# Rows of 1024 floats instead of 1040 for the activations of the second block

## The chip, the cores and the metric

The kernel runs on one core of a Trainium2 chip, as one program on five engines: TensorE (matmuls), ScalarE, VectorE, GpSimd and the queues that issue transfers (SyncE above all). The metric is the device time of one execution in microseconds; before and after are each the median of several executions.

## What is computed

Two transformer blocks follow each other on a sequence of 1024 tokens of 1024 channels, in float32.

```
x = first_block(x, ...)     # 16 meta tokens in front (1040 rows); 2 layers of:
                            #   rmsnorm, h @ w_in, differential and forgetting attention, @ w_out
x = second_block(x, ...)    # 1024 rows; 1 layer of:
  h_lat = modulate(rms_norm(x, g_mix_pre), sh_a, sc_a)
  proj = h_lat @ w_in       # q, k, v, g: retention over 4 heads;  f: 2-D Fourier mix over 4 groups
  mix = concatenate([ret, fourier_mix(f)]) @ w_out
  x = x + gt_a * rms_norm(mix, g_mix_post)
  u = modulate(rms_norm(x, g_ffn_pre), sh_f, sc_f) @ w_up      # 1024 x 1024 @ 1024 x 5632
  a, b = split(depthwise conv of width 3 over u)
  x = x + gt_f * rms_norm((silu(a) * b) @ w_down, g_ffn_post)  # 1024 x 2816 @ 2816 x 1024
```

## The kernel before

Every large product is made in a split form: each float32 operand is stored as a rounded high part and a remainder, both as float32r, and `mm3` (L960) issues three matmuls for each tile, high x high, high x low and low x high, all through `mm` (L957, the matmul itself is L958). On-chip memory holds the activations in two tiles, AH (high) and AL (low), each of 128 partitions x 8 rows x L floats with L = 1040, since the first block has 16 meta tokens before the 1024 tokens. Row k holds channels 128k to 128k+127 (one a partition) for all tokens. Behind AH and AL lie W32 (two slots of 1024 floats, where weights land), WH and WL (two slots of 1024 floats each, their high and low parts), small tiles of 480 floats in all, and then what each block carves for itself: in the Fourier stage YH begins 11,040 floats into that, and YL 5,120 floats after YH. The second block works on 1024 tokens, and uses columns 0 to 1023 of the same AH and AL.

All engines follow one static order. Weights come in the order of a list (`PLAN`): a DMA into W32, ScalarE makes WH, VectorE makes WL, and TensorE waits for the semaphore `w_lo`. PSUM banks are handed out by `banks`. Every stage of the second block that the change touches:

- **Mixer and Fourier input** (`tensor_chunk`, called by `project` in `tensor_mixer` and in `tensor_fourier`): for 16 + 4 weight slices of 128 columns and two halves of 512 tokens, 8 rows k x 3 matmuls. The weight slice is stationary, 512 tokens of row k of AH or AL move. GpSimd (copy into AH) and VectorE (remainder into AL) write the normalised input before.
- **Output projection** (`tensor_out` with the name "out2"): 128 tokens of row k are stationary, 256 columns of the weight move. ScalarE (`hi`) and VectorE (`lo`) write its input.
- **Up-projection** (`tensor_chunk` and, for part of the first slice, `right`, in pieces of 256 tokens): 44 weight slices x two halves of tokens, 24 matmuls each, weight stationary and activations moving. GpSimd and VectorE write the input (`ffn_fill`).
- **Down-projection** (`product`): the gated values n = 0 to 43 (22 rows, for two halves of the output) pass through the eight rows of AH and AL in turn, row `ai = (FT * half + k) % 8`. 128 tokens of that row are stationary, 512 weight columns move. k is the outer loop and the token tile t the inner one, 24 matmuls for a k, except for the last 4 k of the second half, where t is outside.

Between the mixer's products and the output projection stands a Fourier stage (`rows` in `tensor_fourier`) with other tiles, YH and YL, as the stationary operands and WH and WL moving; for each group six matmuls of 512 columns with two of 2 columns between them. The context's projection uses views CAH and CAL of tiles KH and KL. Neither is touched by the change. The first block goes on using AH and AL as they are.

Of the kernel before, what the change touches and what calls it, by code (L numbers as in the profile page):

```python
# [12 lines left out]
SEQ = 1024  # L13
# [79 lines left out]
def build(nc, A, S, O):  # L93

    ctx = ExitStack()
    with ctx:
# [14 lines left out]
        PSf = PS[:, :, :].rearrange("p a b -> p (a b)")  # L111
        AH = sb("AH", [128, KT, L], F32R)
        AL = sb("AL", [128, KT, L], F32R)
        W32 = sb("W32", [128, 2, 1024])
        WH = sb("WH", [128, 2, 1024], F32R)
        WL = sb("WL", [128, 2, 1024], F32R)
# [888 lines left out]
        def tensor_chunk(e, w, key, c, n, freed_by, among, end):  # L1005
            t = split_slot(w)
            wh = WH[:, t, :].rearrange("p (k m) -> p k m", k=KT)
            wl = WL[:, t, :].rearrange("p (k m) -> p k m", k=KT)
            b, free = banks.take(key, freed_by, among)
            for cc, kk in free or ():  # L1010
                e.wait_ge(*cc.at(kk))
            e.wait_ge(*w_lo.at(w))
            for k in range(KT):
                m = mm3(e, bank(b)[:, 0:n], wh[:, k, :], wl[:, k, :], AH[:, k, c:c + n], AL[:, k, c:c + n], k == 0, k == KT - 1)
            m.then_inc(*gemm_mm.mark(key))
            if end:
                W_OVER[w] = (gemm_mm, key)
# [363 lines left out]
        def tensor_fourier(e):  # L1381

            def take(key, freed, among):
                b, free = banks.take(key, freed, among)
                for c, k in free or ():
                    e.wait_ge(*c.at(k))
                return b

            def columns(g, among=ALL):

                out = []
                for nt in range(0, 4, 2):
                    b = take(("cd", g, nt), [(cd_lo, (g, nt))], [x for x in among if x not in out])
                    out.append(b)
                    if g == 0 and nt == 0:
                        e.wait_ge(*cd_in.at("all"))
                    e.wait_ge(*folded.at(g))
                    for i in range(2):
                        c, o = 128 * (nt + i), bank(b)[:, 256 * i:256 * i + 256]
                        mm(e, o[:, 0:128], FTt[:, g, c:c + 128], CD[:, 0:128], True, True)  # L1400
                        m = mm(e, o[:, 128:256], FO[:, g, c:c + 128], CD[:, 128:256], True, True)
                    m.then_inc(*cd_mm.mark((g, nt)))
                return out

            def start_rows(g, among):

                even[g] = take(("even", g), [(es, g)], among[:1])
                odd[g] = take(("odd", g), [(y_v, g)], among[1:])

            def rows(j, g):  # L1410

                w = WI["dft", j]
                s = split_slot(w)
                oe, oo = bank(even[g]), bank(odd[g])
                if j == 0:
                    e.wait_ge(*cd_lo.at((g, 2)))
                if g == 0:
                    e.wait_ge(*w_lo.at(w))
                ah, al = YH[:, j, g, 0:128], YL[:, j, g, 0:128]
                bh, bl = YH[:, j, g, 128:256], YL[:, j, g, 128:256]  # L1420
                mm3(e, oo, bh, bl, WH[:, s, 512:1024], WL[:, s, 512:1024], j == 0, False)
                mm(e, oo[:, 0:2], ah, ALT, False, False)
                mm(e, oo[:, 0:2], al, ALT, False, j == 3)
                m = mm3(e, oe, ah, al, WH[:, s, 0:512], WL[:, s, 0:512], j == 0, j == 3)
                if j == 3 or g == 3:
                    m.then_inc(*dft_mm.mark((j, g)))
                W_OVER[w] = (dft_mm, (j, 3))

            def middle(g):

                e.wait_ge(*fo_out.at(("mid", g)))
                mm(e, bank(even[g]), CD[:, 0:128], F5[:, g, :], False, False)
                mm(e, bank(odd[g])[:, 0:1], CD[:, 0:128], F5[:, g, 0:1], False, False)

            even, odd = {}, {}
            for g in range(4):
                for ci, (c, n) in enumerate(CH2):
                    tensor_chunk(e, WI["fou", g], ("fou", g, ci), c, n, [(fo_out, (g, ci))], ALL, ci == 1)
                    if g and ci == 0:
                        columns(g - 1)  # L1440
            for g in range(3):
                free = sorted((b for b in ALL if b not in list(even.values()) + list(odd.values())), key=lambda b: banks.taken[b])
                start_rows(g, free[:2])
                rows(0, g)
            last = columns(3, [b for b in ALL if b not in list(even.values()) + list(odd.values())])
            for g in range(3):
                rows(1, g)
            start_rows(3, last)
            rows(0, 3)
            rows(1, 3)  # L1450
            for g in range(4):
                middle(g)
            for j in (2, 3):
                for g in range(4):
                    rows(j, g)

            def first(kt):
                return [(y_lo, kt)]
            tensor_out(e, "out2", [128 * t for t in range(8)], first, lambda q, p: (mix_dve, (q, p)),
                       middle=lambda i: tensor_norm_fill(e, "ffn", i - 2, [b for b in ALL if b != banks.place["out2", 2, i]]) if i >= 2 else None)  # L1460
            tensor_norm_fill(e, "ffn", 2, [b for b in ALL if b not in (banks.place["out2", 2, 3], banks.place["out2", 3, 3])])

        def tensor_ffn(e):
            place = {}

            def right(ab, i):
# [8 lines left out]
                wh, wl = (x(w).rearrange("p (k m) -> p k m", k=KT) for x in (high, low))  # L1475
                c = slice(512 + 256 * i, 768 + 256 * i)
                for k in range(KT):
                    m = mm3(e, bank(place[ab])[:, 256 * i:256 * i + 256], wh[:, k, :], wl[:, k, :], AH[:, k, c], AL[:, k, c],
                            k == 0 and i == 0, k == KT - 1)
                if i == 1:  # L1480
                    m.then_inc(*gemm_mm.mark(key))
# [14 lines left out]
            for half in range(2):  # L1496
                held = [banks.take(("down", half, t), [(down_act if t % 2 else down_dve, t)] if half == 0 else None, ALL) for t in range(8)]

                def product(t, k):
# [12 lines left out]
                    if k == 0:  # L1512
                        for c, x in free or ():
                            e.wait_ge(*c.at(x))
                    m = mm3(e, bank(b), AH[:, ai, 128 * t:128 * t + 128], AL[:, ai, 128 * t:128 * t + 128],
                            WH[:, s, wv], WL[:, s, wv], k == 0, k == FT - 1)
                    if k == FT - 1 or t == 7:
                        m.then_inc(*down_mm.mark((half, k, t)))
# [44 lines left out]
        def scalar(e):  # L1563
# [372 lines left out]
            def fourier():  # L1936
# [24 lines left out]
                e.wait_ge(*mx_in.at("all"))  # L1961

                def hi(g, src):
                    e.activation(AH[:, g, 0:SEQ], src, ACT.Copy).then_inc(*y_hi.mark(g))

                for g in range(4):
                    hi(g, MX[:, g, :])
# [69 lines left out]
            def first_rows(side, a=0, b=4):  # L2037

                e.wait_ge(*g_v.at((3, 1)))
                c = slice(512 * side, 512 * side + 512)  # L2040
                for n in range(a, b):
                    e.activation(AH[:, n, c], G[:, n, c], ACT.Copy).then_inc(*g_hi.mark((side, n)))

            def ffn():
                e.wait_ge(*cw_in.at(0))
# [26 lines left out]
                for half in range(2):  # L2072
                    for k in range(FT):
                        if k % 2 == 0:
                            split_to(WI["down", half, k] + 1)
                        while n <= min(FT * half + k + 3, 2 * FT - 1):
                            kk = n % FT
                            if n >= 8:
                                p = n - 8
                                e.wait_ge(*down_mm.at((p // FT, p % FT, 7)))  # L2080
                            e.activation(AH[:, n % 8, 0:SEQ], G[:, kk, :], ACT.Copy).then_inc(*g_hi.mark(n))
                            n += 1
                        if half and 1 <= k <= 8:
                            t = k - 1
# [50 lines left out]
        def vector(e):  # L2135
# [373 lines left out]
            def lat_fill(p):  # L2509
                c = 256 * p  # L2510
                for k in range(KT):
                    e.wait_ge(*lat_hi.at((p, k)))
                    e.tensor_tensor(AL[:, k, c:c + 256], TBc[:, k % 4, :], f(AH[:, k, c:c + 256]), ALU.subtract).then_inc(*fill_lo.mark(("lat", p, k)))  # L2513

            def between_blocks(add, gain):
                add(0)
# [200 lines left out]
            def fourier():  # L2717
# [10 lines left out]

                def lo(g, src):
                    e.wait_ge(*y_hi.at(g))  # L2730
                    e.tensor_tensor(AL[:, g, 0:SEQ], src, f(AH[:, g, 0:SEQ]), ALU.subtract).then_inc(*y_lo.mark(g))

                for g in range(4):
                    split_to(WI["fou", g] + 1)
# [84 lines left out]
            def ffn_fill(p):  # L2819
                for k in range(KT):  # L2820
                    e.wait_ge(*lat_hi.at(("ffn", p, k)))
                    c = 256 * p
                    e.tensor_tensor(AL[:, k, c:c + 256], TBf[:, (8 * p + k) % 4, :], f(AH[:, k, c:c + 256]), ALU.subtract).then_inc(
                        *fill_lo.mark(("ffn", p, k)))

            def first_rows(side, a=0, b=4):
                c = slice(512 * side, 512 * side + 512)
                for n in range(a, b):
                    e.wait_ge(*g_hi.at((side, n)))
                    e.tensor_tensor(AL[:, n, c], G[:, n, c], f(AH[:, n, c]), ALU.subtract).then_inc(*g_lo.mark((side, n)))  # L2830

            def ffn():
                e.wait_ge(*cw_in.at(0))
# [33 lines left out]
                for half in range(2):  # L2867
                    for k in range(FT):
                        if k % 2 == 0:
                            split_to(WI["down", half, k] + 1)  # L2870
                        while n <= min(FT * half + k + 3, 2 * FT - 1):
                            kk = n % FT
                            e.wait_ge(*g_hi.at(n))
                            e.tensor_tensor(AL[:, n % 8, 0:SEQ], G[:, kk, :], f(AH[:, n % 8, 0:SEQ]), ALU.subtract).then_inc(*g_lo.mark(n))
                            n += 1
                        if half and k == 12:
                            gate_rows(GAf, J2f, 1)
# [35 lines left out]
        def gpsimd(e):  # L2913
# [81 lines left out]
            for p in range(4):  # L2995
                for k in range(KT):
                    e.wait_ge(*fill_tb.at(("lat", p, k)))
                    e.tensor_copy(AH[:, k, 256 * p:256 * p + 256], TBc[:, k % 4, :]).then_inc(*lat_hi.mark((p, k)))
            for t in range(8):
                e.wait_ge(*scaled.at(("lat", t)))  # L3000
                e.tensor_scalar(HT[:, t, :], HT[:, t, :], R12[:, 0, t:t + 1], None, ALU.mult).then_inc(*lat_hi.mark(("x0", t)))
# [25 lines left out]
            def ffn_fill(p):  # L3027
                for k in range(KT):
                    e.wait_ge(*fill_tb.at(("ffn", p, k)))
                    e.tensor_copy(AH[:, k, 256 * p:256 * p + 256], TBf[:, (8 * p + k) % 4, :]).then_inc(*lat_hi.mark(("ffn", p, k)))  # L3030

            residual(0)
            residual(1)
# [187 lines left out]
```

## Time and profile before

| | |
|---|---|
| median of 3 runs | 2876.15 us (2875.58 to 2883.48) |
| the profiled execution, its own time | 2872.7 us |
| its span, first to last instruction | 2870.9 us |
| granted TensorE clock, mean over the span | 0.99 |
| second block, roughly | from 1660 us to the end |
| up-projection | 2142 to 2619 us |
| down-projection | from 2619.5 us to the end |

The profile is of one execution. An engine's busy time is the union of its instructions' durations; for matmuls the durations overlap, because they are pipelined and their ends are modelled, and so the distance from one start to the next is what a matmul occupies. In the rows below `PS<-WH,AH` names the output, the moving operand and the stationary operand, in this order.

### The profile page before, as it was taken

Reading aid. Unit: us, or ns where it says so; the run is one execution under the profiler, and the core shown is the slowest. Engines: PE = TensorE matmul, PEld = TensorE weight load, DVE = VectorE, ACT = ScalarE, POOL = GpSimd, SP = SyncE. Lnnn points to the kernel's source line nnn. Section 1 sums busy time; section 2 is a strip of 40 time slices with the busy share of each in tenths; the row PEclk is TensorE's granted clock in tenths of the full one; section 3 lists DMA queues with packets and bytes.
Section 4 is the critical chain, followed back from the end, with each engine's and each line's share of the span. In section 5 each row is a group of like instructions: output and inputs, shape, how many; then the busy total and the mean of one; then the engine's idle time right before and its main releaser. Section 6 shows DMA issues by size and latency. Waiting matters only on the chain.

```text
span 2870.9 us, 43103 instructions
## 1 busy us (share of the span) xinstructions
PE 2785.9 (97%) x17460; PEld 2402.8 (84%) x17460; DVE 1528.2 (53%) x2774; ACT 1044.9 (36%) x1986; POOL 203.8 (7%) x295
## 2 busy tenths in 40 slices
PE   6999999999999999999999989999999999999999
PEld 5888888888899888888888978888998888888887
DVE  5766555555446666644545475553465444444335
ACT  5434333333334444333334561223352222223232
POOL 1100000000001011000002060000030000000000
PEclk9999999999999999999999999999999999999999
DMA  5221222221322122222214122112231111111113
GB/s 135 48 69 50 69 59 59 61 54 62 120 67 60 53 71 69 63 58 72 65 30 146 58 92 78 52 45 95 97 109 52 52 45 52 45 51 45 52 59 139
DMA packets 205396, 198.10 MB, mean 69 GB/s; under 512 B 7286, under 2 KB 181686, under 8 KB 205198
## 3 DMA queue, kind: packets, MB, share of 16 engines
q1 hardware_dynamic: 187344, 134.27, 17.7%
q0 software_dynamic: 17856, 61.07, 5.8%
q8 instruction: 141, 2.31, 0.3%
q14 instruction: 55, 0.45, 0.0%
HBM read 162.73 MB, written 32.58 MB: 68 GB/s over the span
## 4 chain that ended last, share of the span: by engine, by line
PE 88%; DVE 4%; ACT 3%; DMA 2%; issue 1%; POOL 1%; SPq 0%; ACTq 0%; DVEq 0%; POOLq 0%
PE PS L958 84%; PE PS L967 5%; DMA W<-in_w_in 1%; DVE WL L2142 1%; DMA s_os<-OTt 0%; DVE AL L2513 0%; DMA R<-in_k_fg 0%; ACT WH L1577 0%; DVE AL L2185 0%; DVE AL L2403 0%; DVE V L2314 0%; DVE OTt L2397 0%; ACT TMP L1589 0%; ACT L1749 0%; DVE OTt L2388 0%
## 5 line engine op out<-in xcount | busy, mean ns | idle before, releaser
L958 PE MATMUL PS<-AH,WH 128*128 128x512 f32 (+3 forms) x2624 | 976.5, 372 | 23.5 <-DVE AL L2185 7.1
L958 PE MATMUL PS<-AL,WH 128*128 128x512 f32 (+3 forms) x2624 | 918.5, 350 | 0.0
L958 PE MATMUL PS<-AH,WL 128*128 128x512 f32 (+3 forms) x2624 | 916.0, 349 | 0.0
L958 PEld LDWEIGHTS PS<-AH,WH 128*128 128x128 f32 x2624 | 496.2, 189 | 101.1 <-issue 15.0
L958 PEld LDWEIGHTS PS<-AL,WH 128*128 128x128 f32 x2624 | 496.8, 189 | 50.1 <-issue 1.2
L958 PEld LDWEIGHTS PS<-AH,WL 128*128 128x128 f32 x2624 | 495.9, 189 | 43.0
L2142 DVE TENSOR_TENSOR WL<-W,WH 128x1024 fp32r<-128x1024 f32 x184 | 227.5, 1238 | 282.3 <-ACT WH L1577 282.1
L958 PE MATMUL PS<-WH,AH 128*128 128x256 f32 (+1 forms) x1016 | 328.7, 324 | 11.1 <-DVE AL L2403 5.5
L958 PE MATMUL PS<-WH,AL 128*128 128x256 f32 (+1 forms) x1016 | 327.1, 322 | 0.0
L958 PE MATMUL PS<-WL,AH 128*128 128x256 f32 (+1 forms) x1016 | 326.8, 322 | 0.0
L1577 ACT ACTIVATE WH<-W 128x1024 fp32r<-128x1024 f32 x184 | 193.7, 1053 | 244.7 <-PE PS L958 234.7
L2326 DVE TENSOR_REDUCE ST<-PS 128x1 f32<-128x784 f32 (+8 forms) x272 | 187.8, 732 | 122.1 <-PE PS L958 122.1
L1723 ACT ACTIVATE top<-PS,ST 128x784 f32<-128x784 f32 (+8 forms) x272 | 195.0, 723 | 109.6 <-DVE ST L2326 82.4
L958 PEld LDWEIGHTS PS<-WH,AH 128*128 128x128 f32 x1016 | 193.3, 190 | 30.8 <-DVE AL L2403 5.5
L958 PEld LDWEIGHTS PS<-WH,AL 128*128 128x128 f32 x1016 | 193.6, 191 | 15.2
L958 PEld LDWEIGHTS PS<-WL,AH 128*128 128x128 f32 x1016 | 193.5, 190 | 15.0
L967 PE MATMUL PS<-ident,top 128*128 128x128 f32 (+2 forms) x1132 | 178.5, 279 | 7.9 <-DVE V L2314 3.0
L958 PE MATMUL PS<-top,V 128*64 128x256 f32 (+6 forms) x1176 | 181.4, 369 | 0.9 <-DVE top L2360 0.6
L2061 ACT ACTIVATE R<-PS,R 128x512 f32<-128x512 f32 x88 | 68.5, 780 | 299.4 <-PE PS L958 299.4
L1736 ACT ACTIVATE top<-PS 128x512 f32<-128x512 f32 (+2 forms) x177 | 88.9, 508 | 230.7 <-PE PS L967 229.8
L958 PEld LDWEIGHTS PS<-top,V 128*64 128x64 f32 (+3 forms) x1176 | 118.8, 153 | 64.2 <-issue 37.6
L2850 DVE SCALAR_TENSOR_TENSOR R<-PS,R 128x504 f32<-128x504 f32 x88 | 65.4, 743 | 191.8 <-ACT R L2061 191.8
(340 smaller groups left out, 3372.8 us busy)
## 6 DMA issues: line engine op xcount, KB each, us to landing
W<-in_w_in SPq DMA_DIRECT2D x94, 512.0 KB, 7.7
W<-in_w_ada SPq DMA_DIRECT2D x48, 512.0 KB, 3.7
W<-in_w_up SPq DMA_DIRECT2D x44, 512.0 KB, 3.7
W<-in_w_out SPq DMA_DIRECT2D x24, 512.0 KB, 3.5
W<-in_w_down SPq DMA_DIRECT2D x22, 512.0 KB, 3.6
R<-s_xs POOLq DMA_DIRECT2D x16, 512.0 KB, 6.2
s_adap<-AST POOLq DMA_DIRECT2D x48, 128.0 KB, 7.9
top<-in_x SPq DMA_DIRECT2D x8, 512.0 KB, 9.5
```

Source lines behind the costliest of these rows:

```text
L958: return e.matmul(out, lhsT, rhs, start=start, stop=stop, skip_group_check=True)
L967: return e.transpose(out, in_, ident[0:k, 0:k])
L1577: e.activation(high(v), W32[:, s, :], ACT.Copy).then_inc(*w_hi.mark(v))
L1723: e.activation(P[0:rows, P_SLOT[u], 0:W], PSf[0:rows, o:o + W], ACT.Exp, bias=st[:, 0:1], accum_out=st[:, 1:2]).then_inc(*exped.mark(u))
L1736: e.activation(o, i, ACT.Copy).then_inc(*pt_act.mark(key))
L2061: e.activation(dst[:, c:c + n], bank(b), ACT.Identity, scale=CW[:, 1, jj:jj + 1], bias=CW[:, 3, jj:jj + 1]).then_inc(*conv_a.mark((j, ab, ...
L2142: e.tensor_tensor(low(v), W32[:, slot32(v), :], f(high(v)), ALU.subtract).then_inc(*w_lo.mark(v))
L2326: e.tensor_reduce(ST[0:rows, ST_SLOT[u], 0:1], PSf[0:rows, o:o + W], AX.X, ALU.max, negate=True).then_inc(*row_max.mark(u))
L2850: e.scalar_tensor_tensor(d3[:, :, 1:64], o3[:, :, 0:63], CW[:, 0, jj:jj + 1], d3[:, :, 1:64], ALU.mult, ALU.add).then_inc(*conv_v.mark((j, ...
```

## The change

Two views, BH and BL, are made of the memory of AH and AL: beginning 128 floats in, 8 rows of 1024 floats. 128 + 8 x 1024 = 8320 floats, the whole of the tile's 8 x 1040. Every place in the second block that wrote or read AH and AL now uses BH and BL, with the same row numbers and columns; the first block and its views stay as they are. No instruction, wait, transfer or order is added, removed or moved.

```diff
         AH = sb("AH", [128, KT, L], F32R)
         AL = sb("AL", [128, KT, L], F32R)
+        BH, BL = (x[:, :, :].rearrange("p a b -> p (a b)")[:, 128:8320].rearrange("p (a b) -> p a b", a=KT) for x in (AH, AL))
...
@@ tensor_chunk: mixer, Fourier input, up-projection
-                m = mm3(e, bank(b)[:, 0:n], wh[:, k, :], wl[:, k, :], AH[:, k, c:c + n], AL[:, k, c:c + n], k == 0, k == KT - 1)
+                m = mm3(e, bank(b)[:, 0:n], wh[:, k, :], wl[:, k, :], BH[:, k, c:c + n], BL[:, k, c:c + n], k == 0, k == KT - 1)
...
@@ output projection
-            tensor_out(e, "out2", [128 * t for t in range(8)], first, lambda q, p: (mix_dve, (q, p)),
+            tensor_out(e, "out2", [128 * t for t in range(8)], first, lambda q, p: (mix_dve, (q, p)), x=(BH, BL),
...
@@ right(): second half of the first up-projection slice
-                    m = mm3(e, bank(place[ab])[:, 256 * i:256 * i + 256], wh[:, k, :], wl[:, k, :], AH[:, k, c], AL[:, k, c],
+                    m = mm3(e, bank(place[ab])[:, 256 * i:256 * i + 256], wh[:, k, :], wl[:, k, :], BH[:, k, c], BL[:, k, c],
...
@@ product(): down-projection
-                    m = mm3(e, bank(b), AH[:, ai, 128 * t:128 * t + 128], AL[:, ai, 128 * t:128 * t + 128],
+                    m = mm3(e, bank(b), BH[:, ai, 128 * t:128 * t + 128], BL[:, ai, 128 * t:128 * t + 128],
...
@@ the writers, ScalarE, VectorE and GpSimd; one of each
-                            e.activation(AH[:, n % 8, 0:SEQ], G[:, kk, :], ACT.Copy).then_inc(*g_hi.mark(n))
+                            e.activation(BH[:, n % 8, 0:SEQ], G[:, kk, :], ACT.Copy).then_inc(*g_hi.mark(n))
...
-                            e.tensor_tensor(AL[:, n % 8, 0:SEQ], G[:, kk, :], f(AH[:, n % 8, 0:SEQ]), ALU.subtract).then_inc(*g_lo.mark(n))
+                            e.tensor_tensor(BL[:, n % 8, 0:SEQ], G[:, kk, :], f(BH[:, n % 8, 0:SEQ]), ALU.subtract).then_inc(*g_lo.mark(n))
...
-                    e.tensor_copy(AH[:, k, 256 * p:256 * p + 256], TBf[:, (8 * p + k) % 4, :]).then_inc(*lat_hi.mark(("ffn", p, k)))
+                    e.tensor_copy(BH[:, k, 256 * p:256 * p + 256], TBf[:, (8 * p + k) % 4, :]).then_inc(*lat_hi.mark(("ffn", p, k)))
```

## Rows read from the trace of the kernel before

**Rows 1.** The page: span, and busy time of each engine.

```profile
span 2870.9 us, 43103 instructions
PE 2785.9 (97%) x17460; PEld 2402.8 (84%) x17460; DVE 1528.2 (53%) x2774; ACT 1044.9 (36%) x1986; POOL 203.8 (7%) x295
```

**Rows 2.** Busy time by stretch; mixer, output projection with fills, 400 us of the up-projection.

```profile
core 0: us, PE busy (x) PEld busy (x) DVE busy (x) ACT busy (x) POOL busy (x), PEclk, DMA share, GB/s
...
1748.00:1925.00 177.00, 175.97 (x876) 145.85 (x875) 99.96 (x163) 43.03 (x54) 1.60 (x3) 1.00 0.15 45
...
2031.00:2144.00 113.00, 112.45 (x906) 109.85 (x905) 60.80 (x94) 55.75 (x136) 25.54 (x47) 1.00 0.35 117
...
2200.00:2600.00 400.00, 400.00 (x1728) 324.30 (x1727) 191.65 (x217) 109.38 (x126) 0.00 (x0) 1.00 0.16 48
```

**Rows 3.** Waits of TensorE, 1748 us to the end: total, times, longest.

```profile
PE PS L958 <- DVE WL L2142: 1.6, 2, 1.1
PE PS L967 <- ACT R L1898: 1.0, 3, 0.3
PE PS L958 <- ACT R L1923: 0.6, 1, 0.6
```

**Rows 4.** TensorE by form, 1706 us to the end: count | busy us, mean ns.

```profile
L958 PE MATMUL PS<-AH,WH 128*128 128x512 f32 x1008 | 399.7, 396 | 3.0 <-DVE WL L2142 2.9
...
L958 PE MATMUL PS<-WH,AH 128*128 128x512 f32 x352 | 138.6, 394 | 1.2 <-DVE WL L2142 1.1
...
L958 PE MATMUL PS<-WH,AH 128*128 128x256 f32 x192 | 53.9, 281 | 0.4 <-DVE WL L2142 0.4
...
L958 PE MATMUL PS<-EXH,AH 128*128 128x256 f32 x64 | 18.1, 283 | 0.0
...
L958 PE MATMUL PS<-AH,WH 128*128 128x256 f32 x32 | 9.0, 283 | 0.0
```

**Rows 5.** Timeline of TensorE, up-projection: start us, duration us, instruction; twelve matmuls apart.

```profile
2154.53 0.39 PE L958 MATMUL PS<-AH,WH 128*128 128x512 f32 x1
...
2157.31 0.39 PE L958 MATMUL PS<-AH,WH 128*128 128x512 f32 x1
```

**Rows 6.** Timeline of TensorE, down-projection, rows 4 to 7, beginning of row 8.

```profile
2641.62 0.39 PE L958 MATMUL PS<-WH,AH 128*128 128x512 f32 x1
...
2642.99 0.39 PE L958 MATMUL PS<-WH,AH 128*128 128x512 f32 x1
...
2647.07 0.40 PE L958 MATMUL PS<-WH,AH 128*128 128x512 f32 x1
2647.31 0.39 PE L958 MATMUL PS<-WL,AH 128*128 128x512 f32 x1
2647.54 0.40 PE L958 MATMUL PS<-WH,AL 128*128 128x512 f32 x1
...
2652.67 0.39 PE L958 MATMUL PS<-WH,AH 128*128 128x512 f32 x1
...
2658.24 0.39 PE L958 MATMUL PS<-WH,AH 128*128 128x512 f32 x1
...
2663.76 0.39 PE L958 MATMUL PS<-WH,AH 128*128 128x512 f32 x1
```

**Rows 7.** Timeline of TensorE, Fourier stage: two runs of five matmuls each.

```profile
2019.31 0.39 PE L958 MATMUL PS<-WL,YH 128*128 128x512 f32 x1
...
2020.44 0.17 PE L958 MATMUL PS<-ALT,YH 128*128 128x2 f32 x1
...
2020.89 0.40 PE L958 MATMUL PS<-WL,YH 128*128 128x512 f32 x1
...
2022.05 0.17 PE L958 MATMUL PS<-ALT,YH 128*128 128x2 f32 x1
```

**Rows 8.** Timeline of TensorE, output projection of the second block: 24 matmuls apart.

```profile
2034.90 0.28 PE L958 MATMUL PS<-WH,AH 128*128 128x256 f32 x1
...
2037.74 0.28 PE L958 MATMUL PS<-WH,AH 128*128 128x256 f32 x1
```

**Rows 9.** Writers of AL and AH in the down-projection: duration ns min/median/max.

```profile
L2874 DVE TENSOR_TENSOR AL<-R,AH x40: 1216/1218/1227, 2627.7 to 2843.3; 128x1024 fp32r<-128x1024 f32 x40
...
L2081 ACT ACTIVATE AH<-R x40: 1039/1044/1058, 2623.4 to 2842.0; 128x1024 fp32r<-128x1024 f32 x40
```

More of the change, by code:

```diff
@@ L1963, in hi @@
                 def hi(g, src):
-                    e.activation(AH[:, g, 0:SEQ], src, ACT.Copy).then_inc(*y_hi.mark(g))
+                    e.activation(BH[:, g, 0:SEQ], src, ACT.Copy).then_inc(*y_hi.mark(g))
                 for g in range(4):
@@ L2041, in first_rows @@
                 for n in range(a, b):
-                    e.activation(AH[:, n, c], G[:, n, c], ACT.Copy).then_inc(*g_hi.mark((side, n)))
+                    e.activation(BH[:, n, c], G[:, n, c], ACT.Copy).then_inc(*g_hi.mark((side, n)))
             def ffn():
@@ L2512, in lat_fill @@
                     e.wait_ge(*lat_hi.at((p, k)))
-                    e.tensor_tensor(AL[:, k, c:c + 256], TBc[:, k % 4, :], f(AH[:, k, c:c + 256]), ALU.subtract).then_inc(*fill_lo.mark(("lat", p, k)))
+                    e.tensor_tensor(BL[:, k, c:c + 256], TBc[:, k % 4, :], f(BH[:, k, c:c + 256]), ALU.subtract).then_inc(*fill_lo.mark(("lat", p, k)))
             def between_blocks(add, gain):
@@ L2730, in lo @@
                     e.wait_ge(*y_hi.at(g))
-                    e.tensor_tensor(AL[:, g, 0:SEQ], src, f(AH[:, g, 0:SEQ]), ALU.subtract).then_inc(*y_lo.mark(g))
+                    e.tensor_tensor(BL[:, g, 0:SEQ], src, f(BH[:, g, 0:SEQ]), ALU.subtract).then_inc(*y_lo.mark(g))
                 for g in range(4):
@@ L2822, in ffn_fill @@
                     c = 256 * p
-                    e.tensor_tensor(AL[:, k, c:c + 256], TBf[:, (8 * p + k) % 4, :], f(AH[:, k, c:c + 256]), ALU.subtract).then_inc(
+                    e.tensor_tensor(BL[:, k, c:c + 256], TBf[:, (8 * p + k) % 4, :], f(BH[:, k, c:c + 256]), ALU.subtract).then_inc(
                         *fill_lo.mark(("ffn", p, k)))
@@ L2829, in first_rows @@
                     e.wait_ge(*g_hi.at((side, n)))
-                    e.tensor_tensor(AL[:, n, c], G[:, n, c], f(AH[:, n, c]), ALU.subtract).then_inc(*g_lo.mark((side, n)))
+                    e.tensor_tensor(BL[:, n, c], G[:, n, c], f(BH[:, n, c]), ALU.subtract).then_inc(*g_lo.mark((side, n)))
             def ffn():
@@ L2997, in gpsimd @@
                     e.wait_ge(*fill_tb.at(("lat", p, k)))
-                    e.tensor_copy(AH[:, k, 256 * p:256 * p + 256], TBc[:, k % 4, :]).then_inc(*lat_hi.mark((p, k)))
+                    e.tensor_copy(BH[:, k, 256 * p:256 * p + 256], TBc[:, k % 4, :]).then_inc(*lat_hi.mark((p, k)))
             for t in range(8):
```

## The prediction

> **What bounds the kernel now.** I read the page first. TensorE is busy 2785.9 us of a span of 2870.9 us [rows 1]; no other engine comes above 53% there. Then a table of stretches of the second block [rows 2], to see whether that share is a mean over unlike stages. It is not: in the mixer (1748 to 1925 us) TensorE is busy 175.97 of 177 us, in the up-projection 400 of 400 us, and the granted clock is 1.00, the 2.4 GHz level. The table of waits says the same from the other side: from 1748 us to the end TensorE waits 3.2 us in total for anyone [rows 3]. So from there on the span is the sum of the start-to-start distances of matmuls. Only these distances matter, and the change moves no instruction and no wait: whatever it does, it does through the addresses that instructions read and write.
>
> A busy figure can't show that, because a 512-column matmul is drawn with about 395 ns and overlaps its neighbours. The timeline, with a start for each matmul, can. I read it at four places [rows 5 to 8] and divided the distance between two starts by the number of matmuls between them.
>
> **What the change is, in addresses.** A row of AH is 1040 floats, 4160 bytes, which is 16 x 256 + 64. Row k therefore begins 64k bytes past a multiple of 256 from the tile's start: residues 0, 64, 128, 192, 0, and so on, with a period of four rows. A column offset of 128t or 512 floats adds a multiple of 512 bytes and changes nothing. AL lies 33,280 bytes on, 130 x 256, so it has the residues of AH. WH and WL lie 74,752 and 82,944 bytes from AH, both multiples of 256, and their slices of 128, 256 or 512 floats keep residue 0. With the change a row is 4096 bytes and begins 512 bytes in: every operand in BH and BL has residue 0, like the weights. I call that aligned.
>
> **Does an address cost time?** The down-projection answers, because there the activations are stationary, one row k for 24 matmuls in a row, and the rows follow each other with nothing else changing [rows 6]. Row index 4 (aligned) takes from 2641.62 to 2647.07 us, 5.45 us or 227.1 ns a matmul; row 5 takes 5.60 us (233.3 ns), row 6 5.57 us (232.1), row 7 5.52 us (230.0), and then row 8, in place 0 and aligned again, begins. The mean of the four is 22.14 us / 96 = 230.6 ns. Inside the aligned row, the first three matmuls are still uneven; from 2642.99 to 2647.07 us, 18 matmuls take 226.7 ns each. The weights' place (slot and half) has the same period of four, so this alone could be the weights' doing. Two other places speak against that. In the Fourier stage, where stationary YH and YL and moving WH and WL are all aligned (YH lies 137,216 bytes from AH, 536 x 256), five matmuls which go over from one half of the slot to the other take 1.13 us, 226 ns each; after the next pair of two-column products five such take 1.16 us, 232 ns each [rows 7]. So aligned operands can run at 226.7 whichever half is read, but need some matmuls to settle after an interruption. And in the up-projection twelve matmuls, four rows, take 2.78 us, 231.7 ns each [rows 5], the same as over the 400 us with 1,728 matmuls in [rows 2] (one or two of them cut by the edges): the rows' residues repeat every four, while the stationary weight slice moves on by 2048 bytes.
>
> In cycles of 2.4 GHz: 231.7 ns is 556 = 512 x 17/16 + 12, and 226.7 ns is 544 = 512 x 17/16. The 256-column matmuls of the output projection, of which 24 take 2.84 us, 118.3 ns each [rows 8], give 284 = 256 x 17/16 + 12. The same 12 cycles, 5.0 ns, are what the settled aligned stream lacks.
>
> **The sum.** The counts are in [rows 4], each of its rows standing for three equal groups (high x high, low x high, high x low).
> - 512 columns with the activations moving (mixer, Fourier input, up-projection): 1008 x 3 = 3,024 matmuls from 231.7 to 226.7: 15.1 us. No row shows the aligned case in this role with a long run; bounds 0 and 5.0 ns. I take 5.0, since both operands are aligned in [rows 6] and in [rows 7] alike, and the up-projection's 2,016 matmuls (j from 1 on) follow without a gap.
> - 512 columns with the activations stationary (down-projection): 352 x 3 = 1,056 from 230.7 (96 of them are ordered by t at the end, taken at 231.7) to 226.7: 4.2 us, the best founded term.
> - 256 columns: (192 + 64) x 3 in the output projection and 32 x 3 in the first up-projection, 864 in all, from 118.3 to between 118.3 and 113.3: 0 to 4.3 us. I take 4.3 because the excess over 17/16 is the same 12 cycles.
> - Settling: the mixer's and Fourier input's 960 matmuls come in some 21 runs between other products (counted in the code: 2 at the start, 4 for each of three heads, 2 for the last, 5 in the Fourier stage); one settling costs (232 - 226.7) x 5 = 27 ns, together 0.6 us against the above.
>
> Sum: 15.1 + 4.2 + 4.3 - 0.6 = 23.0 us. The fills and splits that write these rows cost nothing extra: VectorE's 40 differences into AL take 1216 to 1227 ns over eight different row starts, and ScalarE's 40 copies 1039 to 1058 [rows 9], so address hardly enters; and they lie beside a TensorE that is busy throughout [rows 2]. If that cover went, 2% of 1.2 us each is nothing either. A row of BH reaches over the head of the next row of AH, but each overwrite of old data is ordered by the waits that stand there today, none added. What is late next if TensorE gains? Per output slice of the up-projection two weights are split and converted on ScalarE and VectorE; in those 400 us VectorE is busy 191.65, ScalarE 109.38, DMA 0.16 of its capacity [rows 2]. A TensorE 2% faster finds all of them ready. In the out-projection to up-projection passage (2031 to 2144 us) VectorE and ScalarE are each busy half of the time, and part of the 4 us may turn into waiting there.
>
> The profiled execution took 2872.7 us, 1.8 over its span, and 3.5 below the median of 2876.15. Taking 23.0 off each gives 2849.7 for such an execution and **2853.2 us** for the median.
>
> The Trainium skill (TensorE: Matmul & The Clock Gate, Single matmul latency and Back-to-back issue gap) gives 215.7 ns for 512 columns; the trace's settled stream has 226.7. By the skill's figure, taken as an estimate for what alignment frees, 4,080 matmuls would save some 65 us and end near 2811; no row comes near it, so I leave it out of the range.
>
> **Rivals.**
> - *Only the stationary role gains.* The down-projection [rows 6] has activations stationary, the up-projection has them moving. If the moving operand's start is what counts in another way there (its rows start 512 bytes into 1024, the weights' do not), the 3,024 keep 231.7. Gain 4.2, with the 256s 4.2 to 7.8: 2868 to 2872. For it: no long aligned run with activations moving exists. Against: [rows 7] moves operands from another half.
> - *The stream does not settle, or only in part.* Interruptions, or copies coming in between, hold it near the 232 of the second five of [rows 7] half of the time: half the gain, 2862 to 2865. Against: 18 even matmuls with the other engines working.
> - *Addresses do not matter, the pattern of four is the weights'.* Two streams read side by side, and neither start slows the other: no change, 2876. For it: the down-projection's weights have the same period. This is also what the Trainium skill says (same page, Part 2): TensorE has two independent read ports, and loading the next weights takes no bandwidth from the running matmul. By that rule all four rows of [rows 6] should take the same, and they differ by 2.7%.
> - *Slower: the aligned stream settles on a slow rhythm.* Row 5 of the down-projection also has a steady rhythm, distances of 0.24 and 0.23 us in turn after 2647.07 us [rows 6], 233.3 ns in the mean. Were that what a uniform stream of moving activations does, 3,024 x 1.6 and 1,056 x 2.6 give 7.6 us, 2884; at 236 ns throughout, 13.0 + 5.6 = 18.6 us, 2895. It decides from 2.1 ns a matmul (8.6 us over 4,080). Against: that rhythm stands at residue 64, the fast one at residue 0.
>
> **Chances.** Full gain 0.76 (own range 2849 to 2858), part 0.06, stationary role only 0.08, no effect 0.05, slower 0.05. The range of 8 in 10 takes the first two: 2849 to 2866. A measurement of this kernel tells 0.3%, 8.6 us, from no change. Below 2867.5 lie the first two and a little of the third: faster 0.84; same 0.11; slower 0.05.
>
> **What would show it.** In the timeline of the up-projection 24 matmuls take 5.44 us instead of 5.56, all distances being 226 or 227, and the stage is 10 us shorter. In the down-projection every row takes 5.44 us. In the output projection twelve matmuls take 1.36 us instead of 1.42. Up to 1706 us nothing moves. Wrong would be: 231.7 kept in the up-projection while the down-projection goes to 226.7 (first rival), or a new wait of TensorE after 2031 us as long as the gain before it.

## The result and the profile after

The changed kernel takes 2857.97 us (median of 6 runs, 2854.23 to 2861.26) against 2875.66 us (6 runs) of the kernel before: 17.7 us less, ratio 0.9935 with a 95% interval of 0.9924 to 0.9946. The forecast was 2853.2 us, with a range of 2849 to 2866.

The page's first lines, of the changed kernel, against [rows 1]:

```profile
span 2859.4 us, 43103 instructions
PE 2773.5 (97%) x17460; PEld 2408.0 (84%) x17460; DVE 1528.1 (53%) x2774; ACT 1044.0 (37%) x1986; POOL 203.5 (7%) x295
```

The same instructions, and the same share of TensorE. Stretches between fixed times, against [rows 2], show the gain only in a count: 400 us of the up-projection now hold 1,766 matmuls instead of 1,728, at the same granted clock. The stretch with the output projection, 2031 to 2144 us, holds 893 instead of 906.

```profile
core 0: us, PE busy (x) PEld busy (x) DVE busy (x) ACT busy (x) POOL busy (x), PEclk, DMA share, GB/s
2200.00:2600.00 400.00, 400.00 (x1766) 331.24 (x1765) 198.04 (x223) 110.67 (x128) 0.00 (x0) 1.00 0.17 49
2031.00:2144.00 113.00, 112.60 (x893) 109.94 (x893) 59.75 (x91) 54.63 (x133) 22.89 (x41) 1.00 0.36 119
```

The waits of TensorE from 1748 us on, against [rows 3], sum to 3.5 us instead of 3.2. The time gained has not turned into waiting.

```profile
PE PS L959 <- DVE WL L2143: 1.5, 2, 1.1
PE PS L968 <- ACT R L1899: 1.4, 4, 0.3
PE PS L959 <- ACT R L1924: 0.6, 1, 0.6
```

The timeline of TensorE in the up-projection, starts twelve matmuls apart, against [rows 5]: 2.72 us for twelve instead of 2.78, 226.7 ns each.

```profile
2399.92 0.39 PE L959 MATMUL PS<-AH,WH 128*128 128x512 f32 x1
...
2402.64 0.39 PE L959 MATMUL PS<-AH,WH 128*128 128x512 f32 x1
...
2405.36 0.39 PE L959 MATMUL PS<-AH,WH 128*128 128x512 f32 x1
```

The down-projection, starts of rows 4 to 8, against [rows 6]: 5.44 us for each row, where there had been 5.45, 5.60, 5.57 and 5.52.

```profile
2633.84 0.39 PE L959 MATMUL PS<-WH,AH 128*128 128x512 f32 x1
...
2639.28 0.39 PE L959 MATMUL PS<-WH,AH 128*128 128x512 f32 x1
...
2644.72 0.39 PE L959 MATMUL PS<-WH,AH 128*128 128x512 f32 x1
...
2650.16 0.39 PE L959 MATMUL PS<-WH,AH 128*128 128x512 f32 x1
...
2655.60 0.39 PE L959 MATMUL PS<-WH,AH 128*128 128x512 f32 x1
```

The output projection, twelve matmuls apart, against [rows 8]: 1.44 us for twelve, 120.0 ns each, where there had been 118.3. It has become slower.

```profile
2049.92 0.28 PE L959 MATMUL PS<-WH,AH 128*128 128x256 f32 x1
...
2051.36 0.28 PE L959 MATMUL PS<-WH,AH 128*128 128x256 f32 x1
...
2052.80 0.28 PE L959 MATMUL PS<-WH,AH 128*128 128x256 f32 x1
```

From the first matmul of one stage to the first of the next, the two traces differ like this (us; the stages are those of the second block, the last one ends with the start of the last matmul):

| stage | before | after | difference | forecast |
|---|---|---|---|---|
| mixer and Fourier | 325.63 | 321.72 | -3.9 | -4.2 |
| output projection and fills | 97.10 | 98.15 | +1.0 | -3.8 |
| up-projection | 491.38 | 481.27 | -10.1 | -10.8 |
| down-projection | 245.07 | 240.93 | -4.1 | -4.2 |
| sum | | | -17.1 | -23.0 |

(The forecast is divided here by where its terms lie: 960 and 2,064 matmuls of 512 columns, 768 and 96 of 256.) The spans of the two profiles differ by 11.5 us only, because in this execution the mixer's first matmul starts at 1710.93 us instead of 1705.37, behind code that the change does not touch. Over the ten traces of this study that start lies between 1701.8 and 1714.5 us, and the stage lengths of equal code repeat within 0.1 us, the mixer's within 1.3. So everything below is read from stages; whole times are compared only where there are several runs.

### The profile page after: what moved, and what is told of

It is laid out like the page before. It is cut to its first block, busy times and chain, and to the rows that moved or that the text cites. A ratio compares the mean times of both kernels' runs of the same rounds, so it can differ in the third digit from the quotient of the medians.

```text
span 2859.4 us, 43103 instructions
## 1 busy us (share of the span) xinstructions
PE 2773.5 (97%) x17460; PEld 2408.0 (84%) x17460; DVE 1528.1 (53%) x2774; ACT 1044.0 (37%) x1986; POOL 203.5 (7%) x295
## 4 chain that ended last, share of the span: by engine, by line
PE 88%; DVE 4%; DMA 3%; ACT 3%; issue 1%; POOL 1%; SPq 0%; ACTq 0%; DVEq 0%; POOLq 0%
PE PS L959 83%; PE PS L968 5%; DMA W<-in_w_in 2%; DVE WL L2143 0%; DMA s_os<-OTt 0%; DVE AL L2514 0%; ACT WH L1578 0%; DMA R<-in_k_fg 0%; DVE AL L2186 0%; DVE AL L2404 0%; DVE OTt L2398 0%; DVE V L2315 0%; ACT TMP L1590 0%; ACT L1750 0%; DVE OTt L2389 0%
## 5 line engine op out<-in xcount | busy, mean ns | idle before, releaser
L959 PE MATMUL PS<-WH,AH 128*128 128x256 f32 (+1 forms) x1016 | 328.9, 324 | 11.5 <-DVE AL L2404 5.4
```

What stands on the lines that cost most here:

```text
L959: return e.matmul(out, lhsT, rhs, start=start, stop=stop, skip_group_check=True)
```

## The experiments

Write d for the start of the moving operand minus that of the stationary operand, modulo 256 bytes (so d is 0, 64, 128 or 192 here; other values were not tried). **Theory A** says that d decides what a matmul in a steady stream takes. **Theory B** says that the absolute place of the activations does, **theory C** that a uniform pitch is enough.

### e1: everything 64 bytes further on

```diff
+        sb("PAD", [128, 16])
         AH = sb("AH", [128, KT, L], F32R)
```

> Theory A, only the distance between the starts of the moving and the stationary operand counts, modulo 256 bytes: everything is shifted by 64 bytes together, so the up-projection keeps 24 matmuls in 5.44 us (226.7 ns each), the down-projection the same, the output projection 120.0 ns; time as of the changed kernel, 2858. Theory B, the absolute place of the activations counts: this is then a kernel with all rows 64 bytes further on, and the down-projection takes the 233.3 ns of row 5 before, the up-projection more than 230 ns; time some 25 us above, 2883. Theory C, only that all rows have the same residue counts: as A.

One run: 2851.9 us. The up-projection, twelve matmuls apart:

```profile
2399.54 0.39 PE L960 MATMUL PS<-AH,WH 128*128 128x512 f32 x1
...
2402.26 0.39 PE L960 MATMUL PS<-AH,WH 128*128 128x512 f32 x1
```

2.72 us again. The up-projection takes 481.31 us, the output projection 98.16, the down-projection 240.93, all as in the changed kernel. Theory B falls: the activations have moved by 64 bytes, together with the weights, and no stage has changed. (The 6 us below the median of the changed kernel lie ahead of the mixer, which starts at 1701.84 us.)

### e2, e3, e4: the same pitch, other distances

The tiles get 64 more floats, so that what lies behind keeps its residue, and the views begin 144, 160 or 176 floats in. With that the activations lie 64, 128 or 192 bytes on from the weights.

```diff
-        BH, BL = (... [:, 128:8320] ... for x in (AH, AL))
...
+        BH, BL = (x[:, 144:8336].rearrange("p (a b) -> p a b", a=KT) for x in (AHt, ALt))   # e3: 160, e4: 176
```

> Rows of 1024 floats, begun 144 floats in (residue 64 against the weights, for all rows). Theory A: the down-projection goes to the 233.3 ns of row 5 before, +7 us against the changed kernel; if the moving role takes the same, the up-projection to 233.3, +20 us; time 2875 to 2888. Theory C (a uniform pitch of 1024 is what frees the time): 226.7 everywhere, 2858.

> Begun 160 floats in (residue 128 for all rows). Theory A: the down-projection goes to the 232.1 ns of row 6 before, +5.7 us against the changed kernel; moving role unknown, between 226.7 and 236; time 2864 to 2888. Theory C: 226.7 everywhere, 2858.

> Begun 176 floats in (residue 192 for all rows). Theory A: the down-projection goes to the 230.0 ns of row 7 before, or 229.3 once settled, +3 us against the changed kernel; moving role between 226.7 and 236; time 2861 to 2888. Theory C: 226.7 everywhere, 2858.

e2: 2867.42 us (10 runs), ratio 0.9978 (0.9967 to 0.9988) to the kernel before, which took 2873.37 us on the same chip (13 runs). e3: 2886.16 us, e4: 2882.99 us, one run each. The down-projection of e2, three row starts and the one of row 8: 5.60 us for each row, also for the rows that had other starts in the kernel before:

```profile
2632.89 0.39 PE L959 MATMUL PS<-WH,AH 128*128 128x512 f32 x1
...
2638.49 0.39 PE L959 MATMUL PS<-WH,AH 128*128 128x512 f32 x1
...
2644.09 0.39 PE L959 MATMUL PS<-WH,AH 128*128 128x512 f32 x1
...
2655.29 0.39 PE L959 MATMUL PS<-WH,AH 128*128 128x512 f32 x1
```

The same 24 matmuls in e3, and in e4, take 5.60 and 5.50 us. Of e3:

```profile
2652.63 0.40 PE L959 MATMUL PS<-WH,AH 128*128 128x512 f32 x1
...
2658.23 0.40 PE L959 MATMUL PS<-WH,AH 128*128 128x512 f32 x1
```

Of e4:

```profile
2653.57 0.39 PE L959 MATMUL PS<-WH,AH 128*128 128x512 f32 x1
...
2659.07 0.39 PE L959 MATMUL PS<-WH,AH 128*128 128x512 f32 x1
```

The up-projection, where the activations move, 24 matmuls from first to last row. Of e2:

```profile
2399.68 0.39 PE L959 MATMUL PS<-AH,WH 128*128 128x512 f32 x1
...
2405.17 0.39 PE L959 MATMUL PS<-AH,WH 128*128 128x512 f32 x1
```

Of e3:

```profile
2400.19 0.39 PE L959 MATMUL PS<-AH,WH 128*128 128x512 f32 x1
...
2405.76 0.40 PE L959 MATMUL PS<-AH,WH 128*128 128x512 f32 x1
```

Of e4:

```profile
2399.89 0.39 PE L959 MATMUL PS<-AH,WH 128*128 128x512 f32 x1
...
2405.49 0.39 PE L959 MATMUL PS<-AH,WH 128*128 128x512 f32 x1
```

Theory C falls: the pitch is 1024 floats in all, and only one of the four starts gives 226.7 ns. The weights' place as the cause of the pattern of four falls too: their slots and halves alternate as before in the down-projection, and the rows are all equal. What remains is d. When the activations move it is their offset, when they are stationary it is minus their offset. In ns for one matmul (24 starts apart in the timeline, so good to some 0.4 ns):

| d | 512 columns, activations moving | 512 columns, activations stationary |
|---|---|---|
| 0 | 226.7 (changed) | 226.7 (changed) |
| 64 | 228.8 (e2) | 229.2 (e4) |
| 128 | 232.1 (e3) | 233.3 (e3) |
| 192 | 233.3 (e4) | 233.3 (e2) |

The two columns agree within 1.2 ns though the roles are exchanged, which the absolute place could not give. In these streams every stationary operand has the same start modulo 256, so the runs do not tell whether d is taken to the stationary operand in use or to the one that is loaded next.

Two expectations missed. e3's down-projection has 233.3 ns, not the 232.1 of row 6 before. And e2 is faster than the kernel before: its up-projection had been put at 233.3 ns by the down-projection's figure, and it took the sign of the distance, seen only here, to explain 228.8. The sign was then used ahead of a run, in e6.

The table also shows what the mixture itself cost. In the up-projection before, d changed every three matmuls, and the stream took 231.7 ns; the mean of the four moving values is 230.2. So of the 5.0 ns gained about 1.5 come from keeping one distance at all, and 3.5 from its being 0. In the down-projection before, d changed only every 24 matmuls, and the mean of 230.6 ns is that of the column on the right, 230.6.

The output projection of e2, twelve matmuls apart, has what the changed kernel lacks:

```profile
2049.79 0.28 PE L959 MATMUL PS<-WH,AH 128*128 128x256 f32 x1
...
2051.15 0.28 PE L959 MATMUL PS<-WH,AH 128*128 128x256 f32 x1
...
2052.51 0.28 PE L959 MATMUL PS<-WH,AH 128*128 128x256 f32 x1
```

1.36 us for twelve, 113.3 ns each, at d = 192. The stage takes 94.11 us there, 4.0 less than in the changed kernel. The other two distances don't come near it. Of e4's output projection (d = 64), 24 matmuls apart, 2.83 us or 117.9 ns each:

```profile
2050.09 0.28 PE L959 MATMUL PS<-WL,AH 128*128 128x256 f32 x1
...
2052.92 0.28 PE L959 MATMUL PS<-WL,AH 128*128 128x256 f32 x1
```

Of e3's (d = 128), 2.88 us or 120.0 ns each (further on in that stage, 118.6):

```profile
2049.96 0.28 PE L959 MATMUL PS<-WL,AH 128*128 128x256 f32 x1
...
2052.84 0.28 PE L959 MATMUL PS<-WL,AH 128*128 128x256 f32 x1
```

### e5: begun 192 floats in

As e2, with 192 in place of 144.

> Rows of 1024 floats, begun 192 floats (768 bytes) in: residue 0 modulo 256 again, another residue modulo 512 and 1024. Theory A (the distance modulo 256 bytes decides): 226.7 ns in the up- and the down-projection, 120.0 in the output projection, as the changed kernel. Rival (the distance modulo 512 or more decides): other values.

One run: 2861.15 us. The output projection takes 98.16 us, the up-projection 481.29, the down-projection 240.93: each within 0.02 us of the changed kernel's. So at d = 0 a further 256 bytes between the operands change nothing: the distance counts modulo 256 bytes.

### e6, e7, e8: the output projections at d = 192

In e6 the moving weights, not the activations, are put elsewhere for one stage.

```diff
+        LATER = {w for key, w in WI.items() if key[0] == "out2" and key[1:] != (0, 0)}
+        def place_of(w):
+            return 1024 * split_slot(w) + (48 if w in LATER else 0)
...
         def high(w):
-            return ASIDE[w][0] if w in ASIDE else WH[:, split_slot(w), :]
+            return ASIDE[w][0] if w in ASIDE else WHt[:, place_of(w):place_of(w) + 1024]
...
-            EXH = spot("EXH", 22304 - 20256, [128, 2, 1024])[:, :, :]
+            EXH = spot("EXH", 22304 - 20256 + 48, [128, 2, 1024])[:, :, :]
```

The low parts are treated alike. e7 has that, and this for the attention outputs and the output projection of the first block's second layer:

```diff
+        DH, DL = (... [:, 80:8272] ... for x in (AH, AL))     # 8 rows of 1024 floats
...
-                    e.activation(AH[:, g, c:c + n], src[:, c:c + n], ACT.Copy).then_inc(*o_hi.mark((l, g)))
+                    e.activation(DH[:, g, 0:SEQ] if l else AH[:, g, c:c + n], src[:, c:c + n], ACT.Copy).then_inc(*o_hi.mark((l, g)))
...
-        OUT_COLS = [[NM + 128 * t for t in range(8)] + [0], [NM + 128 * t for t in range(8)]]
+        OUT_COLS = [[NM + 128 * t for t in range(8)] + [0], [128 * t for t in range(8)]]
```

> The changed kernel, but in the second block's output projection the moving weights lie 48 floats (192 bytes) further on, in 672 of its 768 matmuls (all but those of the first weight). Theory A: moving minus stationary is then 192 as in the kernel begun 144 floats in, and these take 113.7 ns instead of 120.0: 4.2 us less than the changed kernel, 512-column stages unchanged. Rival (at 256 columns the place of the activations alone made the difference): 120.0 stays, no gain.

> The kernel before this one in the list, and in the first block's second layer the attention outputs and the output projection use rows of 1024 floats begun 80 floats in (residue 64: moving minus stationary is 192). Theory A: the 768 matmuls of 256 columns there go from 118.3 to 113.7 ns, another 3.5 us less, 7.7 us less than the changed kernel; the fill after them is not later. Rival: the fills there set the end and the gain turns into waiting.

> The changed kernel itself, for comparison on the same chip: 226.7, 226.7 and 120.0 ns by stage, ratio 0.9935 to the kernel before.

Timed on one chip against the kernel before (2875.92 us, 11 runs), 6 runs each:

| | median us | ratio (95%) | output projection and fills, second block |
|---|---|---|---|
| e8, the changed kernel | 2859.96 | 0.9937 (0.9919 to 0.9955) | 98.16 |
| e6 | 2856.74 | 0.9932 (0.9916 to 0.9949) | 94.54 |
| e7 | 2852.21 | 0.9918 (0.9901 to 0.9934) | 94.54 |

The intervals overlap; between e6, e7 and e8 the whole times tell nothing certain. The stage does: 3.6 us less where 4.2 were expected, the up- and down-projection at 481.28 and 240.93 as before. Of e6, twelve matmuls apart:

```profile
2049.81 0.28 PE L964 MATMUL PS<-WH,AH 128*128 128x256 f32 x1
...
2051.17 0.28 PE L964 MATMUL PS<-WH,AH 128*128 128x256 f32 x1
```

1.36 us. Moving the weights by +192 bytes does what moving the activations by +64 did in e2: theory A at 256 columns too, and the rival (the activations' place alone) falls.

In e7 the first block's output projection has d = 192 as well. Its first 192 matmuls, once they are under way, run as expected, 1.36 us for twelve:

```profile
1566.03 0.28 PE L965 MATMUL PS<-WH,AH 128*128 128x256 f32 x1
...
1567.39 0.28 PE L965 MATMUL PS<-WH,AH 128*128 128x256 f32 x1
```

Then other products come between, and behind them the same stream has another pace:

```profile
1606.04 0.28 PE L965 MATMUL PS<-WH,AH 128*128 128x256 f32 x1
...
1607.45 0.28 PE L965 MATMUL PS<-WH,AH 128*128 128x256 f32 x1
...
1608.87 0.28 PE L965 MATMUL PS<-WH,AH 128*128 128x256 f32 x1
```

2.83 us for 24, 117.9 ns each, and so it stays to the end of the projection. The expected 3.5 us shrink to some 1.1, an estimate: 165 matmuls at the fast rhythm x 5.0 ns and 576 x 0.4. Whether the fills behind set the end, the expectation's rival, can't be told beside that. The same second rhythm is to be seen in e2, at the end of its output projection, after a group of transposes has come between:

```profile
2104.78 0.28 PE L959 MATMUL PS<-EXH,AH 128*128 128x256 f32 x1
...
2106.19 0.28 PE L959 MATMUL PS<-EXH,AH 128*128 128x256 f32 x1
...
2107.61 0.28 PE L959 MATMUL PS<-EXH,AH 128*128 128x256 f32 x1
```

In e6 the same group of 16 transposes comes twice between. After the first the stream goes on at 1.36 us for twelve:

```profile
2105.11 0.28 PE L964 MATMUL PS<-EXH,AH 128*128 128x256 f32 x1
...
2106.47 0.28 PE L964 MATMUL PS<-EXH,AH 128*128 128x256 f32 x1
```

After the second it takes 1.41:

```profile
2117.09 0.28 PE L964 MATMUL PS<-EXH,AH 128*128 128x256 f32 x1
...
2118.50 0.28 PE L964 MATMUL PS<-EXH,AH 128*128 128x256 f32 x1
```

With the activations moving, in the 96 matmuls of 256 columns of e4's up-projection, d is 192 as well, and 24 take 2.83 us (2151.06 to 2153.89 us), 117.9 ns each, again behind transposes.

So at d = 192 and 256 columns there are two steady rhythms, 113.3 and 117.9 ns. Each of these streams keeps the one that it has until something comes between, and an interruption can leave it in either. What decides is not shown. e7's median is 4.5 us below e6's; the estimate above accounts for about 1.1 of that, and the rest is not shown by the stages.

## Why the prediction was right, and where it was off

**The bound.** From the mixer on the time is the sum of the matmuls' start distances: right. TensorE's waits went from 3.2 to 3.5 us, and each stage changed by its matmuls' count times their change, to within 0.3 us when the settling is counted.

**Address and time.** Right, and now shown: with nothing changed but starts, 24 matmuls take from 5.44 to 5.60 us. What was called aligned, residue 0 of each operand, says too much: it is enough that both have the same residue. Only the difference of the two starts counts (e1), modulo 256 bytes (e5). And row 6's 232.1 ns was not a settled value; held at that distance the stream takes 233.3 (e3).

**512 columns, activations moving.** Forecast 15.1 less 0.6 for settling. Measured: the mixer and Fourier stage lost 3.9 us, and of the up-projection's 10.1 practically all is this term. Together 14.0. The size is right. That the value of the stationary role would hold for the moving one was a guess, and the prediction said that no row showed it; that the roles are symmetric was shown only by e2 to e4. So the largest term came true on an argument that its rows did not carry, which is luck in part. The prediction also did not see that about a third of it is the price of changing the distance every three matmuls.

**512 columns, activations stationary.** Forecast 4.2, measured 4.1.

**256 columns.** This term failed, in sign and not only in size: "I take 4.3 because the excess over 17/16 is the same 12 cycles". The excess is the same in the mean over a mixture of distances, and is not what goes away at d = 0. At d = 0 the steady rhythm is 120.0 ns, 1.7 above the mixture, and 864 x 1.7 = 1.5 us are lost where 4.3 were to be gained; the output projection, with 768 of them, shows +1.0. The sign that the prediction had named, twelve matmuls in 1.36 us, did not come: they take 1.44. The lower value exists, 113.3 ns, but at d = 192. The bound of "between 118.3 and 113.3" was also wrong: it excluded a loss, though no row showed a run of 256-column matmuls at one distance. [Rows 8] are a mixture of four distances, and a mean says nothing of its parts.

**The sum.** The stages lost 17.1 us where 23.0 were forecast. Of the 5.9 between, 4.8 lie in the output projection and 0.6 in the 96 matmuls of 256 columns in the up-projection; the other terms are off by 0.5 together. The measured time, 2857.97 us, lies at the upper edge of what the prediction had called the full gain, 2849 to 2858: the range holds because the failed term was small beside the two right ones.

**The rivals.** "Only the stationary role gains" is excluded by the up-projection's 226.7. "Addresses do not matter" is excluded by e2 to e4; by the Trainium skill (TensorE: Matmul & The Clock Gate, Part 2: What happens when you issue a matmul) loading the next weights takes no read bandwidth from the running matmul. The traces do not fit this for float32r: the distance between the two operands' starts changes a matmul by up to 6.6 ns of 226.7. "Settles on a slow rhythm" did not happen at 512 columns and did at 256, where it is the +1.7 ns. By the Trainium skill (same page, Back-to-back issue gap) an isolated matmul of 512 columns would take about 216 ns; no stage here, with float32r, reached it: 226.7 is the least. In the first rival the sum is off: 4.2 with the 4.3 of the 256s is 8.5, not 7.8; nothing rests on it.

**Cover.** The writers kept their price: the VectorE differences into the eight rows take a median of 1218 ns as in [rows 9].

## What to carry to other kernels

Where TensorE is busy without a gap, measure start to start, not busy time, and look whether the distance has a period in the loop; a period of four rows was worth 17 us here, for one line of views and their names in the places that use them. Choose row pitch and tile starts so that the moving and the stationary operand keep one distance modulo 256 bytes over the whole loop, then measure which distance is best for that width: of the four tried here, 0 for 512 columns, and 192 for 256, there with a second rhythm that can take most of the gain. A mean over mixed cases bounds none of them from either side.

## What the runs showed of the hardware

In a dense float32r stream at the 2.4 GHz level (granted clock 1.00) one matmul of 512 columns takes from 226.7 to 233.3 ns by the distance of its operands' starts alone (226.7 at 0, 233.3 at 192). One of 256 columns takes from 113.3 to 120.0 (113.3 at 192, 120.0 at 0). The fastest values are 544 and 272 cycles, 17/16 of the column count, at both widths. Streams that changed the distance every three matmuls took 231.7 and 118.3 ns, both 12 cycles above that. At one distance two rhythms can be steady (113.3 and 117.9 ns at 192). Why the time depends on the distance between the two starts, and why the best distance differs with the width, stays open: the runs show the dependence, not its mechanism.
